# An encoder block in one program: VectorE's order in the expert values, one-hot weighing on two engines, and a stage without loops

## The reference, cut to what matters

```python
q = (xt @ wq).reshape(T, 8, 2, 128)                      # 8 heads, two half keys
s = einsum('thpe,hpke->thpk', q, keys)                   # 128 keys per half
sv, si = top_k(s, 16)                                    # 16 of 128, each half
cand = sv[:, :, 0, :, None] + sv[:, :, 1, None, :]       # 16 x 16 sums
tv, ti = top_k(cand, 16);  g = softmax(tv)               # 16 experts of 128*128 per head
a = einsum('cd,ced->ce', xb, utab[ib])                   # token times expert row of utab
coef = g * gelu(a)
out = einsum('ce,ced->cd', coef, vtab[ib])               # weighted sum of rows of vtab
x = LN(alpha * x + (1 + g2) * out)
```

## Time and profile before

| | us |
|---|---|
| median of three runs | 4256.4 |
| the profiled execution, its own time | 4264.03 |
| its span in the trace | 4262.2 |
| TensorE busy | 3770.9 (88%) |
| TensorE weight loads busy | 3277.4 (77%) |
| VectorE busy | 2565.5 (60%) |
| ScalarE busy | 1396.8 (33%) |
| GpSimd busy | 1153.5 (27%) |
| mean granted clock | 0.937 |

### The profile page before, as it was taken

How to read it: one execution, slowest core, us unless ns; L and a number is a source line. 1 busy time by engine, 2 the same in 40 slices (tenths; PEclk the granted TensorE clock), 3 DMA queues, 4 the chain that set the end, 5 groups by cost and what they waited for, 6 DMA issues and landing times. The chain is left out here.

```text
span 4262.2 us, 57381 instructions
## 1 busy us (share of the span) xinstructions
PE 3770.9 (88%) x19170; PEld 3277.4 (77%) x19170; DVE 2565.5 (60%) x5465; ACT 1396.8 (33%) x2897; POOL 1153.5 (27%) x797
## 2 busy tenths in 40 slices
PE   6889899998879798999989889896888988898896
PEld 3579788886657687999988879896677777777775
DVE  5563133224544413999988778785766666666667
ACT  1110122221123211233278888796211111111111
POOL 1132121112322021333343333332323232323330
PEclk9789999998989899999999999898999999999998
DMA  4741212215543222333379999999867677777773
GB/s 176 285 148 40 81 65 81 76 61 217 197 147 124 79 80 90 130 131 132 119 249 329 305 313 322 294 333 304 293 241 238 238 240 244 236 244 246 242 256 136
DMA packets 502745, 826.90 MB, mean 194 GB/s; under 512 B 289175, under 2 KB 309911, under 8 KB 496440
## 3 DMA queue, kind: packets, MB, share of 16 engines
q1 hardware_dynamic: 111848, 370.03, 24.8%
q0 software_dynamic: 84096, 318.80, 21.2%
q10 hardware_dynamic: 306576, 135.28, 12.7%
HBM read 679.31 MB, written 144.70 MB: 193 GB/s over the span
## 5 line engine op out<-in xcount | busy, mean ns | idle before, releaser
L79 PE MATMUL va_fps<-va_vt_h,va_c_h 128*128 128x512 f32 x1536 | 631.1, 411 | 184.6 <-DVE va_vt_l L2204 176.0
L80 PE MATMUL va_fps<-va_vt_l,va_c_h 128*128 128x512 f32 x1536 | 621.9, 405 | 0.0
L81 PE MATMUL va_fps<-va_vt_h,va_c_l 128*128 128x512 f32 x1536 | 621.0, 404 | 0.0
L2082 POOL DMA_INDIRECT va_rows<-in_vtab,k_pick x256 | 377.3, 1474 | 850.4 <-DVE k_big L2228 748.0
L79 PEld LDWEIGHTS va_fps<-va_vt_h,va_c_h 128*128 128x128 f32 x1536 | 305.6, 199 | 262.9 <-issue 164.6
L1916 ACT ACTIVATE ga_first<-ga_first,ga_gs 128x128 f16<-128x128 f16 x1536 | 470.2, 398 | 85.0 <-DVE ga_first L1975 84.8
L79 PE MATMUL ga_aps<-k_u_h,k_ut_h 128*128 128x384 f32 x1152 | 404.6, 351 | 27.9 <-issue 20.8
L81 PE MATMUL ga_aps<-k_u_h,k_ut_l 128*128 128x384 f32 x1152 | 391.7, 340 | 8.0 <-issue 8.0
L80 PE MATMUL ga_aps<-k_u_l,k_ut_h 128*128 128x384 f32 x1152 | 391.3, 340 | 0.0
L2171 ACT ACTIVATE va_c_h<-va_c 128x768 fp32r<-128x768 f32 x128 | 108.1, 845 | 790.1 <-DVE va_c L2196 790.1
L80 PEld LDWEIGHTS va_fps<-va_vt_l,va_c_h 128*128 128x128 f32 x1536 | 305.7, 199 | 64.2
(11 more groups left out here) (295 smaller groups left out, 8078.0 us busy)
## 6 DMA issues: line engine op xcount, KB each, us to landing
k_ut<-in_utab SPq DMA_DIRECT2D x129, 512.0 KB, 5.5
va_vt<-in_vtab SPq DMA_DIRECT2D x128, 512.0 KB, 4.9
va_c<-scratch_ahead SPq DMA_DIRECT2D x128, 384.0 KB, 3.1
va_wt<-scratch_gates SPq DMA_DIRECT2D x128, 384.0 KB, 3.8
hy_tab<-in_tab POOLq DMA_DIRECT2D x64, 512.0 KB, 4.7
scratch_ahead<-ga_gelu_a ACTq DMA_DIRECT2D x72, 384.0 KB, 6.5
sp_wada<-in_w_ada SPq DMA_DIRECT2D x24, 1024.0 KB, 8.6
scratch_gates<-ga_wide ACTq DMA_DIRECT2D x32, 768.0 KB, 14.3
```

The lines of the kernel that those rows point to most:

```text
L79: nc.tensor.matmul(out, w[0], x[0], start=first, stop=False)
L80: nc.tensor.matmul(out, w[0], x[1], start=False, stop=False)
L81: return nc.tensor.matmul(out, w[1], x[0], start=False, stop=last)
L2082: nc.gpsimd.indirect_dma_start(got[:, q % SLOTS_G, :], None, vrows, picked(K, q)).then_inc(got_in[q % SLOTS_G], 16)
```

## The change

In `stage_gates` `TURNS` becomes 1, and the loops of TensorE and VectorE become Python loops, so their programs are written out in full and the operands have fixed addresses. Of the four tokens of a group, ScalarE weighs only tokens 2 and 3 (`BY_ACT`). For tokens 0 and 1 VectorE compares and multiplies with the gate in one pass each for the high and the low gate.

In `stage_values` the order within a turn changes. Rows are no longer taken in equal numbers after each expert's low parts, but ahead of them and at the end of the turn, by `cuts`: with two rows an expert 1, 1, 2, 1 and 3 at the end; with three 1, 2, 3, 2 and 4. The first add of a passing tile stands behind expert 0's low parts, the second behind expert 2's, the third at the very end of the turn.

```diff
-        TURNS = 4
+        TURNS = 1
+        BY_ACT = (2, 3)
...
-            with pe.Fori(0, TURNS) as i:
+            for i in range(TURNS):
...
                 for part in (1, 0):
-                    for t in range(G):
+                    for t in BY_ACT:
...
             def one_hot(m, b):
                 dve.wait_ge(mm, m + 1)
                 for t in range(G):
-                    at = bass.ds(m * G + t, 1)
+                    at = slice(m * G + t, m * G + t + 1)
                     v.tensor_scalar(second[:, b, t, :], iota[:, :], K["sel"][:, 1, at], None, ALU.is_equal)
-                    last = v.tensor_scalar(first[:, b, 0, t, :], iota[:, :], K["sel"][:, 0, at], None, ALU.is_equal)
+                    if t in BY_ACT:
+                        last = v.tensor_scalar(first[:, b, 0, t, :], iota[:, :], K["sel"][:, 0, at], None, ALU.is_equal)
+                        continue
+                    for part in range(2):
+                        v.tensor_scalar(first[:, b, part, t, :], iota[:, :], K["sel"][:, 0, at],
+                                        gs[:, part, at], ALU.is_equal, ALU.mult)
                 last.then_inc(hot_ok, 1)
...
-            with dve.Fori(0, TURNS) as i:
+            for i in range(TURNS):
...
             def turn(s, g, add, start, take):
 
+                cuts = (0, take // 2, take, 2 * take, 3 * take - 1, GT * take)
+
+                def take_rows(place):
+                    for j in range(cuts[place], cuts[place + 1]):
+                        take_row(start, j, isinstance(start, int) and start == 0 and j < GATHERED)
+
                 for t in range(GT):
                     coefficients(g + 1, t)
-                    if t < STAY:
-                        add(t)
+                    take_rows(t)
                     coef_low(1 - s, g + 1, t)
                     value_low(1 - s, g + 1, t)
-                    for j in range(take * t, take * t + take):
-                        take_row(start, j, isinstance(start, int) and start == 0 and j < GATHERED)
+                    if t == 0:
+                        add(0)
+                    if t == 2:
+                        add(1)
+                take_rows(GT)
+                add(2)
```

More of the change, by code:

```diff
@@ L1980, in dot @@
                 dve.wait_ge(got_in[k], 16 * (turn + 1))
-                at = bass.ds(SLOTS_G // GATHERED * turn + k // GATHERED, 1)
+                at = slice(SLOTS_G // GATHERED * turn + k // GATHERED, SLOTS_G // GATHERED * turn + k // GATHERED + 1)
                 v.scalar_tensor_tensor(out=got[k], in0=got[k], scalar=1.0, in1=K["u_row"][:, k % GATHERED, :], op0=ALU.mult,
```

## The result

The changed kernel takes 4092.5 us (median of 4 runs, 4085.7 to 4101.5); the kernel before, beside it, 4260.4. The ratio is 0.9608, with a 95% interval of 0.9584 to 0.9633: 168 us less where 247 were forecast, and 2.5 us above the upper end of the range. The sign and the larger mechanism were right, and one of the two stages gave nothing.

What follows compares the result with a forecast made beforehand. TensorE, stalled by VectorE's queue order, bounds the values stage; three engines near their limit bound the gates stage. Savings of 184 (values) and 63 (gates) from 4256.4 gave 4009 us; 8-in-10 range 3960 to 4090.

Steps and rivals of the forecast that it cites:

- What bounds the kernel: Values stage: TensorE's, stalled 4.4 us a group by VectorE's queue order; gates stage: three engines near their limit.
- The body of the values stage: Values stage: reordered turn cuts a group from 39.3 to 32.8 us, 188 us over 29 groups.
- Rival 2: Values stage: the next wait is near, groups stay at 35.5 us, kernel 4087 us; chance 0.11.
- rival 4: Values stage: the reorder does nothing, the stall moves to passing tiles awaiting adds; kernel 4193 us; chance 0.03.
- The edges of the values stage: Values stage ends: first group loses 3 us, last turn gains 5, four 12-row groups lose 6 to 8 together.
- The price of the pass with two [P,1] operands: Gates stage, VectorE: each new one-hot pass costs 0.16 us; 384 added passes make +63 us, 701 busy.
- The upper bound of 0.284: Gates stage: new passes at 0.284 us at most would add 157 us, VectorE at 795, no gain there.
- Rival 3: Gates stage: two-operand passes leave the fast path; 0.53 us each eats the values gain, 0.7 gives 4390; chance 0.03.
- The price of a loop boundary: Gates stage: each loop boundary costs about 17 us; removing three takes 51 us off, 795 to 744.
- The sharing of the weighing: Gates stage: splitting the weighing between ScalarE and VectorE brings a tile from 10.3 to 10.1 us.
- ScalarE's own relief: Gates stage: 768 fewer weighing copies take 235 us off ScalarE's 672 us of work, leaving 437.
- rival 1: Gates stage stays full of DMA or VectorE, gaining 0 to 20 us; added one-hots may delay GpSimd; 4062 us; chance 0.20.

Runs made afterwards that it cites:

- e1: The kernel before with only the new order of the turn in the values stage; 4086.4 us, ratio 0.9592.
- e2: The changed kernel, without loops, with ScalarE weighing all four tokens again; 4070.0 us, gates stage 765.1 us.
- v1: e2 with first turn in old order and 8 rows, 12-row turns spread 3, 2, 3, 2, 2, four rows in the last turn; 4049.2 us.
- p1: The changed kernel with the second scalar of the 768 new one-hot passes made a constant; 4058.6 us, gates stage 771.4 us.
- e3: The changed kernel with the loops of TensorE and VectorE back, weighing still shared; 4109.4 us, gates stage 812.4 us.
- h1: e2 with gathered rows half as wide (zeros in the other half), dots at full width; 4029.1 us, gates stage 740.9 us.
- p5: The changed kernel with both the gathered rows and their dots at half width; 4000.4 us, gates stage 704.9 us.
- l1: p5 with the loops of TensorE and VectorE back, four turns; 4024.3 us, gates stage 729.1 us.
- p2: The changed kernel with dots of gathered rows over half their columns, same bytes gathered; 4055.7 us, gates stage 759.1 us.

## Why the prediction was wrong

**What bounds the kernel: right.** The values stage was TensorE's with one stall a group.

**The body of the values stage: right, step by step.** 25 groups of 32.6 us, 166.4 us less where 6.5 us a group made 162. The clock came with it, 0.99 for 0.93. `vt` lands later than in the earlier trace rows, 6.9 us at the median for 4.9, and rows too, 7.0 for 5.9, and both stay inside the slacks that were worked out. Rival 2 (35.5 us a group) and rival 4 are refuted.

**The edges of the values stage: mis-sized by some 20 us.** "The first group pays [...] I estimate 3 us" was 12.5, and the four groups next to the first and to the last two lost not 6 but 17 of the 26 us that their share of the 188 had promised them. The step that failed is that I counted the rows as VectorE time (1.2 us each) and as bytes, and not as a chain: row done, buffer free, GpSimd's gather, landing, row. With four rows behind the last low part and four buffers, the last of them wait 3.2 to 5.7 us for their transfer, and `add` stands behind them. Before and e1 together show it for the first group, 12.0 us by the order alone; e2 and v1 give 10.2 us back.

**The price of the pass with two [P,1] operands: the step that failed in the gates stage.** "I take 0.16: it is the same instruction, type and shape". It is 0.22; 768 x 0.223 - 384 x 0.163 = 109 us added, where 63 stood in the sum (the busy time rose by 103). The upper bound of 0.284 and its consequence, no gain in this stage, stood in the prediction, and p1 shows that the operand is the cause. (That bound was a duration set beside a distance between starts, 0.16; the new passes last 0.35 us at the mean and start 0.22 apart, so it held for the distance by luck. Rival 3 needed 0.53 us.) VectorE was then busy 741 us of a stage that was to take 732. That alone refutes the forecast.

**The price of a loop boundary: mis-sized by a factor of two.** "A boundary costs about 17 us, three cost 51": the stop is that long, but 8.1 us each remain in a stage bounded by TensorE, 9.6 in e2's and 6.5 in e3's. I had taken the loss inside the window for the loss of the stage.

**The sharing of the weighing: the sign was wrong.** It was to bring a tile from 10.3 to 10.1 us. It costs 27.8 us. ScalarE did not set the stage alone: e2 leaves it at 670 us of 765, and the same work of ScalarE fits in 741 (h1). With ScalarE weighing, the transfers cost 24 us of the stage by h1 (31 without its zeroing), and behind them ScalarE's own work comes; the transfers were in the prediction as "slightly over the best window" at 341 GB/s, and no kernel here reached more than 326 over the stage. So even with the pass at 0.16 the stage would have stopped at 771 (p1).

ScalarE's own relief was nearly as forecast, 213 us for 235, and was worth nothing. GpSimd's side of rival 1 does not show: its busy time went from 295 to 317 us, and the gathered rows kept nobody waiting for long.

The sum of it: 62 us from the gates stage and 18 from the values stage, of the 83 by which the time missed; the other 3 to 4 are the kernel before, 4260.4 us here and 4256.4 in the prediction. Rival 1 named the place and the engine, "The gates stage stays full of DMA or VectorE". Its 4062 was 30 too low: 18 for the values stage, which it left as forecast, and 9 for a gain in the gates stage that did not come. A chance of 0.20 was too small for it, with a DMA share of 1.07 over the whole stage in the earlier trace rows and 0.1 us a tile of room for VectorE in my own sum.

## What to carry to other kernels

Work moved from one engine to another is priced at the receiving engine with the operation's full form, each operand counted; where a trace shows no such form, the range of the stage must be carried into the likeliest time, not only into a rival. Removing a wait or a stop is worth only the distance to the next limit, and when three engines and the DMA all stand at 80% or more, that distance is a few per cent: relieve two at once in an experiment (as p5) before believing in the third. And in a software pipeline over few buffers, count a gathered row as a chain of buffer, issue and landing; its place in the turn matters more than its time on the engine.

## What the runs showed of the hardware

- A `tensor_scalar` on 128 elements of 16-bit data costs 0.163 us with one [P,1] operand, with or without a second operation on a constant, and 0.22 us with two [P,1] operands.
- The first back jump of the stage stops TensorE for 4.2 and 2.0 us in l1, and for 7.0 and 2.4 in the kernel before; straight code of the same work, four times as long, shows no such stop.
- All kernels that moved all bytes of the gates stage ran at 305 to 326 GB/s with a DMA share of 1.05 to 1.10 in the windows view, and once VectorE was relieved the transfers held the stage there (p2 against p5). Neither bytes per second nor the share alone tells whether they hold a stage: with a quarter of the bytes gone the share was still 0.92 to 1.02 at 230 to 257 GB/s, and at 1.02 the stage was TensorE's (p5). The packets of the changed kernel's gates stage, most of them below 512 bytes, are in the row at the end.
- With under 10 us of waits in them, TensorE had a mean granted clock of 0.99 over the 954 us of the values stage's middle, so its upper level, 2.4 GHz, for nearly all of them.

```profile
DMA packets 304381, 248.11 MB, mean 312 GB/s; under 512 B 253105, under 2 KB 253233, under 8 KB 304305
```
